# One product of summed squares in place of eight, behind the last head of a decoder trunk

## What is computed

```python
def rms_norm(x, g):
    xf = x.astype(jnp.float32)
    y = xf * lax.rsqrt(jnp.mean(xf * xf, axis=-1, keepdims=True) + EPS)
    return (y * g.astype(jnp.float32)).astype(x.dtype)

def conv_ffn(x, norm_g, w_in, dw_w, dw_b, w_out):
    h = rms_norm(x, norm_g)
    u = causal_depthwise_conv(h @ w_in, dw_w, dw_b)
    gate, up = u[..., :D_FF], u[..., D_FF:]
    return x + (jax.nn.silu(gate) * up) @ w_out

        x = x + (o.reshape(b, s, N_HEADS * V_DIM) @ w_o[j].astype(jnp.float32)).astype(x.dtype)
        x = conv_ffn(x, ffn_norm_g[layer], ffn_w_in[layer], ffn_dw_w[layer], ffn_dw_b[layer], ffn_w_out[layer])
```

## Time and profile before

| what | value |
|---|---|
| runs, median (lowest to highest) | 1205.17 us (1204.52 to 1206.13) |
| the profiled execution, its time | 1204.15 us |
| the profiled execution, first to last instruction | 1202.4 us |
| TensorE's mean granted clock | 0.994 of full speed |
| TensorE matmuls busy | 1181.3 us, 98% |
| VectorE busy | 809.4 us, 67% |
| ScalarE busy | 506.2 us, 42% |

### The profile page before, as it was taken

The page is one execution under the profiler, slowest core; times in us unless marked ns, Lnnn a source line. Parts: engine busy times, 40 slices in busy tenths (PEclk is TensorE's granted clock), DMA queues, the critical chain, the costliest instruction groups (busy, mean ns, idle before and its releaser), DMA issues.

```text
span 1202.4 us, 16317 instructions
## 1 busy us (share of the span) xinstructions
PE 1181.3 (98%) x6030; PEld 996.0 (83%) x6030; DVE 809.4 (67%) x1122; ACT 506.2 (42%) x814; POOL 62.8 (5%) x76
## 2 busy tenths in 40 slices
PE   8999979999999999999999999999999999999998
PEld 6888768888888888887999999886888888888887
DVE  6999984676537663667567777876676457653763
ACT  6332354444214431344656666555444124421441
POOL 1000002000000000001212022200000000000000
PEclk9999979999999999999999999999999999999999
DMA  8555712233322333222321221221233322332222
GB/s 294 150 119 123 193 53 70 71 105 105 105 93 82 105 105 105 70 87 87 123 85 41 71 71 49 84 79 36 70 105 105 105 76 100 105 105 85 90 79 96
DMA packets 34614, 116.77 MB, mean 97 GB/s; under 512 B 18304, under 2 KB 18432, under 8 KB 21888
## 3 DMA queue, kind: packets, MB, share of 16 engines
q1 hardware_dynamic: 34560, 116.03, 30.8%
HBM read 109.60 MB, written 6.49 MB: 97 GB/s over the span
## 4 chain that ended last, share of the span: by engine, by line
PE 86%; DVE 7%; ACT 3%; DMA 1%; issue 1%; POOL 0%; SPq 0%; DVEq 0%; POOLq 0%; ACTq 0%
PE bank L1328 72%; PE bank L1489 8%; PE bank L1405 2%; DMA w_raw<-stream 1%; PE bank L1539 1%; PE bank L1523 1%; DVE w_lo L863 1%; ACT prob L817 1%; DVE w_lo L855 1%; ACT w_hi L576 1%; DVE small L1252 1%; PE bank L1367 1%; DVE dT_lo L1244 1%; DVE conv_c L946 1%; PE bank L1508 0%
## 5 line engine op out<-in xcount | busy, mean ns | idle before, releaser
L1328 PE MATMUL bank<-xg_hi,w_hi 128*128 128x512 f32 x832 | 326.7, 393 | 2.8 <-DVE xg_lo L871 2.8
L1328 PE MATMUL bank<-xg_hi,w_lo 128*128 128x512 f32 x832 | 323.8, 389 | 0.0
L1328 PE MATMUL bank<-xg_lo,w_hi 128*128 128x512 f32 x832 | 323.8, 389 | 0.0
L576 ACT ACTIVATE w_hi<-w_raw 128x2048 fp32r<-128x2048 f32 x79 | 150.6, 1907 | 151.4 <-PE bank L1328 147.1
L855 DVE TENSOR_TENSOR w_lo<-w_raw,w_hi 128x2048 fp32r<-128x2048 f32 x79 | 182.7, 2312 | 25.4 <-ACT w_hi L576 25.4
L1328 PEld LDWEIGHTS bank<-xg_hi,w_hi 128*128 128x128 f32 x832 | 156.2, 188 | 37.3 <-DVE xg_lo L871 2.1
L732 ACT ACTIVATE ffn_t<-ffn_u,par 128x512 f32<-128x512 f32 x88 | 72.0, 818 | 268.7 <-DVE ffn_u L1142 268.7
L1328 PEld LDWEIGHTS bank<-xg_lo,w_hi 128*128 128x128 f32 x832 | 156.2, 188 | 33.7 <-issue 1.7
L1328 PEld LDWEIGHTS bank<-xg_hi,w_lo 128*128 128x128 f32 x832 | 156.2, 188 | 32.7
L1328 PE MATMUL bank<-act_hi,w_hi 128*128 128x512 f32 x448 | 177.2, 396 | 4.2 <-DVE act_lo L1072 3.9
L1328 PE MATMUL bank<-act_hi,w_lo 128*128 128x512 f32 x448 | 175.2, 391 | 0.0
(11 more groups left out here) (177 smaller groups left out, 1421.3 us busy)
## 6 DMA issues: line engine op xcount, KB each, us to landing
w_raw<-stream SPq DMA_DIRECT2D x87, 1024.0 KB, 4.9
band_sb<-band SPq DMA_DIRECT2D x12, 512.0 KB, 7.0
w_raw<-stream SPq DMA_DIRECT2D x8, 768.0 KB, 4.2
band<-band_sb SPq DMA_DIRECT2D x4, 1056.0 KB, 12.1
x<-x_t SPq DMA_DIRECT2D x8, 256.0 KB, 6.3
w_raw<-band SPq DMA_DIRECT2D x4, 512.0 KB, 6.1
out_t<-x SPq DMA_DIRECT2D x8, 256.0 KB, 2.0
w_raw<-stream SPq DMA_DIRECT2D x2, 512.0 KB, 5.0
```

The costliest lines, as they stand in the source:

```text
L576: act.activation(w_hi[:, j, :], w_raw[:, j, :], ACT.Copy).then_inc(w_hi_done, 1)
L1328: got = pe.matmul(out, weights(w, j, k, m), v[:, k, :], start=(k == first and s == 0), stop=(k == last and s == 2), skip_group_check=True)
```

## The change

ScalarE writes the eight squares into eight buffers (`sq_all`), so it no longer waits for TensorE. VectorE adds them up in `sq_sum`: squares 0 and 1 behind residual tile 3, the other six behind the last `xg_lo`. The eight products of ones are gone. One product, `square_sum(3)`, stands in the second unit behind m = 0, k = 3.

```diff
-SQUARE_AT = {0: 4, 2: 5, 4: 6, 5: 7}
...
+        sq_all, at = put("sq_all", at, [P, KT, SEQ])
...
-                    xg_tile("ffn1", k)
+                    xg_tile("ffn1", k, square=False)
+                    act.activation(sq_all[:, k, :], x[:, k, :], ACT.Square).then_inc(sq_done, 1)
...
+            def add_residual_square(k):
+
+                at = SQ["ffn1"]
+                dve.wait_ge(sq_done, at + k + 1)
+                if k > 1:
+                    dve.wait_ge(sq_added, 2 + at + k)
+                dve.tensor_tensor(sq_sum, sq_sum if k > 1 else sq_all[:, 0, :], sq_all[:, k, :],
+                                  ALU.add).then_inc(sq_added, 2 if k == 1 else 1)
...
                     if k == 3:
+                        add_residual_square(1)
                         split_rest(0)
                 xg_lo_tile("ffn1", KT - 1)
+                for k in range(2, KT):
+                    add_residual_square(k)
                 split_rest(1)
...
-            def square_add(k):
-
-                pe.wait_ge(sq_done, SQ["ffn1"] + k + 1)
-                pe.matmul(bank[NORM][:, :], ones[:, :], sq[:, k % 2, :], start=(k == 0), stop=(k == KT - 1),
-                          skip_group_check=True).then_inc(norm_mm if k == KT - 1 else sq_added, 1)
...
-                            unit(n0, 0, hi, lo, KT, 2, xg_ready("ffn1"), each=lambda k: k in SQUARE_AT and square_add(SQUARE_AT[k]))
-                        unit(n0 + 1, 1, hi, lo, KT)
+                            unit(n0, 0, hi, lo, KT, 2, xg_ready("ffn1"))
+                        unit(n0 + 1, 1, hi, lo, KT, between=(lambda: square_sum(3)) if layer else None, at=3)
...
             for m in range(3):
-                if m == 2:
-                    square_add(0)
-                    square_add(1)
                 passes(bank[WO_LAST[m]][:, :], m // 2, m % 2, KT - 1, act_hi, act_lo, PART, KT - 1).then_inc(tiles, 1)
...
             got.then_inc(tiles, 1)
-            square_add(2)
-            square_add(3)
             ffn(1)
```

More of the change, by code:

```diff
@@ L1334, in begin, with unit @@
                 pe.wait_ge(banks_free, n + 1)
-            def unit(n, j, hi, lo, count, late=0, ready=None, between=None, at=None, begun=False, each=None):
+            def unit(n, j, hi, lo, count, late=0, ready=None, between=None, at=None, begun=False):
                 if begun:
@@ L1356, in unit @@
                         between()
-                    if each and m == 0:
-                        each(k)
             def square_sum(stage_n):
```

## The result

| | time, us | ratio to before, 95% interval |
|---|---|---|
| before | 1204.85 (4 runs, 1204.27 to 1206.13) | |
| changed | 1212.38 (4 runs, 1211.97 to 1214.91) | 1.0061 (1.0049 to 1.0074) |
| forecast | 1211.2 (1208.4 to 1213.4) | |

A forecast was written before the change was run, and what follows sets the result against it. TensorE was taken as the bound, its matmuls busy for 98% of the span. Terms -6.0 + 2.2 + 7.8 + 2.0 = +6.0 us put the median at 1211.2 us, range 1208.4 to 1213.4.

The forecast's parts named there:

- Seven products, -6.0 us: On TensorE, seven of eight products of squares go, 0.86 us each: -6.0 us.
- First wait, +2.2 us: Ahead of the first feed-forward unit, TensorE idles for banks_free behind residual tile 5: +2.2 us, bounds 0 to 3.4.
- The second unit for nothing: At the second unit, VectorE's six adds and w_lo end by 845.4, before TensorE arrives at 845.7: no cost.
- Third unit's wait, +7.8 us: Ahead of the third unit, TensorE waits for w_lo, 4.2 and 11.7 us behind the later product: +7.8 us.
- The clock, +2.0 us: Behind the third unit's wait, TensorE's granted clock falls to 0.50: +2.0 us, bounds 0 to 2.5.
- The number: Whole kernel: terms sum to +6.0 us, profiled execution 1210.2 us, median 1211.2, range 1208.4 to 1213.4.
- The marks: Signs in the profile after: reciprocal ends near 853.5, third unit's w_lo near 865; wrong if second unit begins behind 846.
- The held clock: Rival: both waits come but TensorE's clock does not fall, 1209.2 us; chance 0.13.
- a start without the first wait: Rival: banks_free is there at 832.6, so the first unit starts 2.2 us earlier, 1209.0 us; chance 0.06.
- The late adds: Rival: VectorE's adds run at GpSimd's pace and hold the second unit 3 us more, 1214.2 us; chance 0.03.
- The faster case: Rival: only the removed products count, 1199.2 us, decided by w_lo at the third unit's start; chance 0.06.
- The page on the clock: Skill page's rule against idle gaps between matmul bursts: with the clock's term +6.0 us, by the rows alone possibly +4.0.

The follow-up runs named there:

- e1: Changed kernel with the banks counted as they come free, three of four counts behind residual tile 1, the last behind tile 7: 1210.61 us, ratio 1.0041.
- e2: Changed kernel with the one product moved from the second unit to the first, behind m = 1, k = 5: 1207.65 us, ratio 1.0018.
- e3: Changed kernel with the one product four groups of three matmuls later in the second unit, behind m = 0, k = 7: 1215.44 us, ratio 1.0076.
- e8: Changed kernel with the third unit's w_lo moved ahead of the first unit's last subtraction on VectorE: 1211.02 us, ratio 1.0045.
- e4: Changed kernel without VectorE's seven adds, the product taking the first square alone: 1213.68 us, ratio 1.0062.
- e5: Changed kernel with nine idle products of ones filling TensorE's wait ahead of the third unit: 1210.45 us, ratio 1.0035.
- e10: Changed kernel with banks counted as they come free, product in first unit behind m = 1, k = 6, third unit's w_lo sooner on VectorE: 1205.19 us.
- e6: Changed kernel with seven idle identity products filling TensorE's wait ahead of the first unit: 1211.94 us, ratio 1.0050.
- e7: Changed kernel with adds on GpSimd, banks counted as they come free, product in the first unit, third unit's w_lo sooner on VectorE: 1205.38 us.

## Why the prediction was right, point by point

- *Seven products, -6.0 us.* Fourteen matmul records are gone and the one product left takes 0.87 us. Right.
- *First wait, +2.2 us.* 2.23 us, on tile 5: it ends at 834.68, and the unit starts at 834.83. e1 showed that it was the count behind tile 5. On the way there `w_lo` started at 831.87, as I wrote, but 831.28 + 0.69 makes 831.97: consecutive rows of VectorE overlap by some 0.1 us.
- *The second unit for nothing.* Its `w_lo` was ready at 844.2, and the product behind its first twelve matmuls started at 850.04 without a wait.
- *Third unit's wait, +7.8 us.* 7.77 us. The chain is 11.70 us long, the product's place sets its start (e2, e3), and its length sets its end (e8).
- *The clock, +2.0 us.* This term was mis-sized: 4.1 us in the changed kernel's profile. I gave the fall to the long wait alone, where it cost 2.5, my upper bound. I missed that the 2.2 us ahead of the first unit would bring it down as well, for 1.6 more; no row of before had shown that a wait of this length is harmless. The pause around 822 us that left the clock alone, which I called some microseconds long, is 1.24 us in the first row of the result.
- *The number.* The sum was +6.0 and the profile has +8.3, just over the +8.2 that the range's upper end leaves above 1205.17. The medians differ by 7.5 us, which is inside. Of the 2.2 us of room above the sum only 0.5 were for the clock, the term that failed by 2.1; the rest was kept for a first wait of up to 3.4 us and for the spread. That the time still lay in the range is luck in part. The bounds that I gave for the forecast's own range also add up to 1210.7 and 1212.9, not to 1210 and 1212.6.
- *The marks.* The second unit began behind 846, at about 847.3, which I had named as a sign of error. It was the clock in the first unit, the same miss, and everything behind it lay some 1.7 us later than I wrote: the reciprocal ended at 855.2, not 853.5, and `w_lo` at 867.0, not 865.2.
- *The rivals.* The held clock is out, and so is a start without the first wait. The late adds are out: six took 4.67 us, and e4 shows no gain without them. The faster case failed where I had put its decision, at the third unit's `w_lo`.
- *The page on the clock.* The rule of the Trainium skill's "TensorE: Matmul & The Clock Gate" (section "HAM oscillation — how this bites in real kernels"), to leave no long idle gaps between bursts of matmuls, agrees with this trace at the third unit: the clock was at 0.50 behind the 7.8 us. That it was at 0.50 behind the 2.2 us as well is more than this rule says, since it speaks of longer gaps.

## What to carry to other kernels

Before work is taken off the busiest engine, ask when its result is needed: here the product moved from inside the first unit to inside the second, and a chain of 15.9 us behind it, hidden until then, came to lie on TensorE's path. Cheaper products at nearly the old place won 4 us over the kernel before, where fewer products at a later place lost 7.5. A wait also has a second price where it takes TensorE's clock down, and a counter that several units share can hold back one whose own banks have long been free.

## What was not expected of the hardware

**The clock falls in short waits, but not in all.** Waits of TensorE of 2.0 to 2.5 us behind dense matmuls were followed by a granted clock of 0.50 in the profiles of the changed kernel, e2 (twice), e3, e4, e5 and e10. In e8 the first wait was 2.2 us as well, and the first unit ran at 1.00 (the columns of the windows above):

```profile
834.00:836.00 2.00, 0.10 (x1) 1.00 0.63 115
836.00:838.00 2.00, 2.00 (x9) 1.00 0.88 365
```

So the same wait costs 1.6 us more in one execution than in another. The kernel's start shows it too: ahead of 12 us TensorE waits for one of its first `xg_lo`, 2.0 to 2.3 us in e5, e8 and e10 with a fall behind it, and 2.4 us in e6 with none (e8, then e6):

```profile
12.00:16.00 4.00, 4.00 (x12) 0.62 1.04 426
```

```profile
12.00:16.00 4.00, 4.00 (x18) 1.00 1.03 421
```

The scatter of the runs goes with the granted clock: e5's shortest run, 1208.2 us, had a mean of 0.995 and its longest, 1213.53, 0.990. Which falls made the difference has not been traced.

**GpSimd's adds slow some of VectorE's instructions and not others.** In e7 those with two tiles in SBUF became longer, up to about twice, while the residual's add, with one operand in PSUM, kept its 0.68 us. The Trainium skill's page "SBUF — State Buffer" (section "Who interferes with whom") says just this: a VectorE instruction with two SBUF inputs contends with a GpSimd instruction that reads SBUF, since its second input comes through the read port that the two share. In the expectation of e7 I had left that as an aside, and it took most of the gain: 3.8 us of waits, of which e1 has only 0.3, against the products' 6.0.
